# Cached pages loaded with two neighbouring tokens on each partition, the two pages of a block on alternate partitions

## The chip, the cores and the metric

The kernel runs on one core of a Trainium2 chip. The metric is the device time of one execution in microseconds (us). The two timed executions of the kernel before gave 888.59 and 891.32 us, a median of 889.96 us.

## What is computed

One inference step of a one-layer decoder with eight attention heads of 64 and four pooling groups. A prompt of 512 tokens and eight sample sequences of four new tokens each go through the same layer. What bears on this change is the attention of the samples: each sequence has 4096 past tokens in a paged cache, 32 pages of 128 tokens, found through a page table. Two pages form a block of 256 tokens. For each head and query the mean of the keys of a block gates it, the best three of the 16 past blocks are attended, and a relative-position bias is added, which depends on the distance of query and key.

```
past = cache_k[layer, page_table[:, :own * ppb]]            # 8 sequences x 32 pages x 128 tokens x 8 heads x 64
kmean = jnp.mean(past.reshape(DB, own, MOBA_BLOCK, N_HEADS, HEAD_DIM), axis=2)
gate = jnp.einsum('bhtd,bhnd->bhtn', qh, kmean)
_, sel = lax.top_k(gate, n_sel)                              # 3 of 16 blocks
s_sel = einsum('bhcd,bhcnkd->bhcnk', qc, k_sel) * SCALE + bias_tab[h_ix, t5_bucket(rel_s)]
p = softmax(concat([s_sel, s_own]))
out = einsum(p_sel, v_sel) + einsum(p_own, v_own)
```

The bias is bucketed. A key more than 127 or so tokens away falls in the last bucket (31), so of the 32 past pages only the last one has biases that differ from token to token. The sum over keys doesn't depend on the order in which the keys of a page stand, as long as keys, values and biases stand in the same one.

## The kernel before

All arrays are float32. The program has a start (modulation, projections, lines 1060 to 1320 on the engines), the attention of the prompt, the output projection of the prompt, and then the MLP of the prompt in eight chunks of 512 hidden columns, beside which the eight sample sequences' attention runs: while the MLP's chunk `i` is worked on, TensorE scores the keys of one sequence, weighs the values of another, and the loads of a third are under way. Five rounds of this are a hardware loop (`Fori(0, LAST - 2)`); the round before it and those after it are written out. At the end the samples' own MLP runs with weights loaded a second time, 2 MB at a time ("tail" pieces).

The cached pages come through SyncE's queue. `load_block` reads two page numbers from the table, waits until a slot of a ring is free, and issues one DMA for each of the two pages, [128 partitions x 512] each: a partition holds one token, 8 heads x 64, 2048 bytes. There are four slots (`SLOTS`) of two pages (`PPB`) for keys (`k_ring`, in `rw`) and four for values (`v_ring`, in `W`). All 512 such DMAs share one queue with the weights: quarters of `w_up` ([128 x 8 x 128]) and `w_down` ([128 x 4 x 256]), and the tail pieces. A slot of keys is free when VectorE has turned it (`kt_ev`), a slot of values when TensorE has weighed it (`v_used`).

VectorE turns each page of keys in 32x32 squares (`turn_keys`, one STREAM_TRANSPOSE [128 x 512] for each page), TensorE multiplies four pages at a time with the queries (`score_keys`), so that in `sc` a row of 128 lanes (head or query group) holds 1024 columns of scores, 32 for each page and quarter. `scores_out` takes them out of PSUM in two halves, adds the far bias `farr` (one number for each lane) to all columns but the last page's, and `lastr` to those of the last page, columns 480 to 511 of the second half. ScalarE takes the exponential, TensorE turns the probabilities and weighs the values page by page (`weigh_values`).

`lastr` is made once, near the start: TensorE multiplies one-hot bucket rows (the table `last` in the constants `c32`) with the relative-bias table into PSUM bank 4, VectorE masks by quarter and reduces over the four quarters (`bias_out_of_banks`). The constants come to `const32`, 32 partitions of 1536 columns, in one DMA issued from line 455.

The order of the queue is written out by hand: `section(i, u)` issues for each eighth of a round two blocks of keys, two of values and one quarter of weights, each behind its wait.

Of the kernel before, what the change touches and what calls it, by code (L numbers as in the profile page):

```python
# [17 lines left out]
ALU = mybir.AluOpType  # L18
# [3 lines left out]
P = 128  # L22
# [4 lines left out]
DB, DT = 8, 4  # L27
NS = DB * DT
# [11 lines left out]
PPB = 2  # L40
# [10 lines left out]
REV = 2 * P + P - 1  # L51
C32 = {}
_at = 0
for _name, _n in (("ownmask", DB * NS), ("rev", REV + 1), ("far", P), ("last", DT * P), ("own", DT * NS), ("spread", P)):
    C32[_name] = (_at, _at + _n)
    _at += _n
C32_W = _at
# [13 lines left out]
def bucket(n):  # L71
    n = max(n, 0)
    if n < 16:
        return n
    return min(16 + int(math.log(n / 16) / math.log(8) * 16), 31)


def shape_constants():

    c128 = np.zeros((P, C128_W), np.float32)  # L80
    part = {name: c128[:, lo:hi] for name, (lo, hi) in C128.items()}
    part["ident"][:] = np.eye(P)
    part["flip"][:] = np.eye(P)[::-1]
    for g, w in enumerate(WINDOWS):
        part["inv_count"][:, 16 * g:16 * g + 16] = 1.0 / np.minimum(np.arange(16) + 1, w)
    for p in range(P):
        h, g, t = p // 16, p // DT % QUADS, p % DT
        part["fold"][p, p % HT] = 1.0
        part["head"][p, p % HT // DT] = 1.0
        part["token"][p, p % DT] = 1.0  # L90
        part["quad"][p, g] = 1.0
        part["others"][p, 0] = NEG if g else 0.0
        for x in range(QUADS):
            part["same"][p, h * 16 + x * DT + t] = 1.0
            part["cross"][p, x * HT + h * DT + t] = 1.0
        for c in range(CUTS):
            part["qmask"][p, c * 2 * QUADS + c // 2 % 2 * QUADS + p // 32] = 1.0
    for n in range(BLOCKS):
        part["lower"][:, n * BLOCKS:n * BLOCKS + n] = 1.0
    c32 = np.zeros((32, C32_W), np.float32)  # L100
    cmask = np.zeros((NH, REV), np.float32)
    o = C32["rev"][0]
    for i in range(REV):
        rel = 2 * P - 1 - i
        if rel >= 0:
            c32[bucket(rel), o + i] = 1.0
        else:
            cmask[:, i] = NEG
    c32[31, C32["far"][0]:C32["far"][1]] = 1.0
    o = C32["last"][0]  # L110
    for t in range(DT):
        for key in range(P):
            c32[bucket(P + t - key), o + t * P + key] = 1.0
    o = C32["own"][0]
    for t in range(DT):
        for r in range(NS):
            c32[bucket(t - r % DT), o + t * NS + r] = 1.0
    o = C32["spread"][0]
    for r in range(HT):
        c32[r, o + r // DT * 16 + r % DT] = 1.0  # L120
    o = C32["ownmask"][0]
    for row in range(HT):
        for b in range(DB):
            for key in range(NS):
                if key // DT != b or key % DT > row % DT:
                    c32[row, o + b * NS + key] = NEG
    return c128, c32, cmask


def decoder_step(nc, x_prompt, x_sample, cache_k, cache_v, state_pool, page_table, c_prompt, c_sample, w_ada, b_ada,  # L130
# [4 lines left out]
    with ctx:  # L135
        def sb(name, shape, dt=F32):
            return ctx.enter_context(nc.sbuf_tensor(name, shape, dt))
# [69 lines left out]
        rstds = sb("rstds", [P, NS])  # L207
        farb = sb("farb", [P, NH])
        farr = sb("farr", [P, 1])
        lastr = sb("lastr", [P, 32])  # L210
        own = sb("own", [P, DB, NS])
        owncur = sb("owncur", [P, NS])
        ownb = sb("ownb", [HT, NS])
# [31 lines left out]
        c_tok = rw[0:1 + DB, 0:D]  # L245
        vec_rows = rw[0:VECS, 2 * D:2 * D + P]
        st_rows = rw[0:DB * STATE, 2304:2304 + AW]
        const32 = rw[0:32, 3072:3072 + C32_W]
        bias_rows = rw[0:NH, 4864:4864 + REV]
        mask_rows = rw[0:NH, 5376:5376 + REV]  # L250
        relb = rw[0:32, 5888:5888 + NH]
# [2 lines left out]
        relx = rw[0:32, 6144:6144 + 5 * P].rearrange("p (s h g t) -> p s h g t", s=5, h=NH, g=QUADS)  # L254
        relrows = rw[0:32, 6144:6144 + 5 * P].rearrange("p (s r) -> p s r", s=5)
        relown = rw[0:32, 6912:6912 + DT * HT].rearrange("p (s h t) -> p s h t", s=DT, h=NH)
        near_last = cmps[:, 0:P].rearrange("p (g n) -> p g n", g=QUADS)
        ada_sums = [rw[:, 7168:7168 + PIECE], rstd[:, :]]
        qT = gT
        v_tok = rw[:, 0:2048].rearrange("p (t n) -> p t n", t=TT)  # L260
# [16 lines left out]
        def bank(i, parts=P, n=512, off=0):  # L277
            return PS[0:parts, i, off:off + n]
# [165 lines left out]
        def _(sp):  # L444
# [47 lines left out]
            def load_block(cache, ring, landed, b, j, freed=None):  # L492

                slot = j % SLOTS
                _, phys = nc.values_load_multi_w_load_instructions(pages[0:1, bass.ds(b * PAGES + PPB * j, PPB)],
                                                                   engines=[mybir.EngineType.SP])
                if freed:
                    sp.wait_ge(*freed)
                for pg in range(PPB):
                    sp.dma_start(ring[:, slot, pg, :], cache[bass.ds(phys[pg], 1), :, :].rearrange("a p n -> (a p) n"))\  # L500
                      .then_inc(landed[slot], 16)

            def load_keys(b, j, first=False):
# [559 lines left out]
        def _(dve):  # L1063
# [112 lines left out]
            def bias_out_of_banks():  # L1176

                dve.wait_ge(bias_ps, 2)
                dve.tensor_copy(farb[:, :], bank(4, P, NH)).then_inc(bias_ev, 1)
                dve.tensor_copy(farr[:, :], bank(4, P, 1, 16)).then_inc(bias_ev, 1)  # L1180
                dve.tensor_tensor(near_last, bank(4, P, P, P).rearrange("p (g n) -> p g n", g=QUADS),
                                  own_quad[:, :, None].to_broadcast([P, QUADS, 32]), ALU.mult).then_inc(last_raw, 1)
                dve.tensor_copy(ownb[:, :], bank(4, HT, NS, 64)).then_inc(bias_ev, 1)
                dve.wait_ge(last_raw, 1)
                dve.tensor_reduce(lastr[:, :], near_last.rearrange("p g n -> p n g"), AX.X, ALU.add).then_inc(bias_ev, 1)
# [153 lines left out]
            def scores_out(b, half):  # L1339

                dve.wait_ge(qk, UNITS * b + 4 * (half + 1))
                src = bank(2 + half)
                lo, mid, hi = 512 * half, 512 * half + (480 if half else 512), 512 * half + 512
                dve.tensor_reduce(gsum[:, 8 * half:8 * half + 8], src.rearrange("p (u n) -> p u n", u=8), AX.X, ALU.add)
                ins = dve.tensor_scalar(sc[:, lo:mid], src[:, 0:mid - lo], farr[:, 0:1], None, ALU.add)
                if half:
                    ins = dve.tensor_tensor(sc[:, mid:hi], src[:, mid - lo:512], lastr[:, :], ALU.add)
                ins.then_inc(sc_in, 1)
                dve.wait_ge(sc_in, 2 * b + half + 1)
                dve.tensor_reduce(tops[:, 8 * half:8 * half + 8], sc[:, lo:hi].rearrange("p (u n) -> p u n", u=8),  # L1350
                                  AX.X, ALU.max).then_inc(sc_ev, 1)
# [206 lines left out]
        def _(pe):  # L1558
            def mm(out, lhsT, rhs, start=True, stop=True, **kw):
                return pe.matmul(out, lhsT, rhs, start=start, stop=stop, **kw)  # L1560
# [86 lines left out]
                lo = C32["own"][0] + t * NS  # L1647
                mm(bank(4, HT, NS, 64), relown[:, t, :, :].rearrange("p h t -> p (h t)"), const32[:, lo:lo + NS], t == 0, t == DT - 1)
            for t in range(DT):
                lo = C32["last"][0] + t * P  # L1650
                last = mm(bank(4, P, P, P), relrows[:, t, :], const32[:, lo:lo + P], t == 0, t == DT - 1)
            last.then_inc(bias_ps, 1)


# [545 lines left out]
```

## Time and profile of the kernel before

| | |
|---|---|
| timed executions, median (lowest to highest) | 889.96 us (888.59 to 891.32) |
| profiled execution, its time | 896.14 us |
| its span, first to last instruction | 894.3 us |
| mean granted TensorE clock | 0.98 |
| TensorE busy | 838.0 us (94%) |
| VectorE, ScalarE, GpSimd busy | 448.7, 338.0, 292.6 us |
| moved by DMA | 254.02 MB, 284 GB/s on the mean |
| the hardware loop, one round | 66.77 us |

The profiled execution's span is 4 us above the median of the timed ones, so differences are what is carried from one to the other. TensorE's busy time is modelled at the ends of its matmuls; what shows its pace is how long a round of the loop takes. "DMA share" is the mean share of time in which the 16 DMA engines had a packet under way; packets overlap a little, so that it can pass 1.

### The profile page before, as it was taken

What the parts mean: (1) busy time and instruction counts of PE and PEld (TensorE: products, weight loads), DVE (VectorE), ACT (ScalarE), POOL (GpSimd) and SP (SyncE); (2) the same over time, 40 slices, a digit from 0 to 9 for tenths busy, and PEclk for the clock granted to TensorE, in tenths of its full rate; (3) what the DMA queues carried; (4) which work ended last, traced back from release to release, by engine and by line L of the source; (5) the groups of instructions that cost most, each with busy time, mean ns of one, the idle gap of its engine ahead of it and who ended that gap; (6) DMA issues with size and microseconds to landing.
All of it is one profiled execution on the core that took longest, in us unless ns stands there. A gap on an engine that the chain in (4) does not pass through costs nothing.

```text
span 894.3 us, 20195 instructions
## 1 busy us (share of the span) xinstructions
PE 838.0 (94%) x7634; PEld 589.7 (66%) x7634; DVE 448.7 (50%) x845; ACT 338.0 (38%) x701; POOL 292.6 (33%) x191
## 2 busy tenths in 40 slices
PE   5799999898999699999999999999999999997984
PEld 4577786666776176666666676676676675576873
DVE  2743223664777884674674674674674441221222
ACT  4233223787114646136136136036036145133011
POOL 0330003956132444334334334334333353225000
PEclk9899999999999899999999999999999999999998
DMA  9842236595998889999999999999999999899896
GB/s 302 324 154 95 95 115 253 166 337 177 297 312 262 298 279 309 316 315 321 311 316 329 299 321 323 302 310 326 298 325 364 288 309 333 279 326 329 304 397 248
DMA packets 167825, 254.02 MB, mean 284 GB/s; under 512 B 10454, under 2 KB 69419, under 8 KB 167755
## 3 DMA queue, kind: packets, MB, share of 16 engines
q1 hardware_dynamic: 166995, 250.66, 82.9%
q0 software_dynamic: 768, 2.51, 0.8%
q8 instruction: 43, 0.70, 0.3%
q14 instruction: 19, 0.16, 0.0%
HBM read 248.56 MB, written 4.75 MB: 283 GB/s over the span
## 4 chain that ended last, share of the span: by engine, by line
PE 80%; DMA 7%; DVE 6%; issue 2%; ACT 2%; SPq 2%; POOL 0%; DVEq 0%; ACTq 0%
PE PS L1560 77%; DMA W<-in_w_down_dram 3%; DMA W<-in_cache_v_dram 2%; DMA mixT<-in_x_prompt_dram 1%; SPq L500 1%; DMA out_dram<-hT 1%; DVE W L1337 1%; PE PS L1909 1%; PE PS L1783 1%; DMA W<-in_w_up_dram 1%; DVE hT L1116 1%; DVE xT L1405 1%; DVE mixT L1277 0%; DVE stat L1279 0%; POOL hT_split L644 0%
## 5 line engine op out<-in xcount | busy, mean ns | idle before, releaser
L706 POOL TENSOR_TENSOR W_split<-W,W_split 128x1024 fp32r<-128x1024 f32 x72 | 172.3, 2393 | 298.6 <-ACT W_split L866 143.2
L1560 PE MATMUL PS<-gT_split,W_split 128*128 128x512 f32 x576 | 200.9, 408 | 1.0 <-DVE xT L1405 0.2
L1337 DVE STREAM_TRANSPOSE W<-rwT 128x512 f32<-128x512 f32 x256 | 162.6, 681 | 36.5 <-PE PS L1560 22.6
L1560 PE MATMUL PS<-rwT_split,W_split 128*128 128x512 f32 x512 | 175.0, 404 | 0.0
L1560 PE MATMUL PS<-hT_split,W_split 128*128 128x512 f32 x416 | 162.3, 399 | 0.5 <-ACT mixT L939 0.5
L1560 PEld LDWEIGHTS PS<-gT_split,W_split 128*128 128x128 f32 x576 | 109.1, 189 | 53.9 <-DVE xT L1405 17.2
L1560 PEld LDWEIGHTS PS<-rwT_split,W_split 128*128 128x128 f32 x512 | 96.7, 189 | 31.9 <-issue 12.6
L1405 DVE SCALAR_TENSOR_TENSOR xT<-PS,mods,xT 128x512 f32<-128x512 f32 x64 | 47.5, 742 | 110.5 <-PE PS L1560 110.2
L866 ACT ACTIVATE W_split<-W 128x1024 fp32r<-128x1024 f32 x32 | 33.9, 1059 | 179.7 <-DMA W<-in_w_up_dram 179.6
L1560 PE MATMUL PS<-kT_split,W_split 128*128 128x512 f32 x256 | 100.3, 392 | 0.0
L1560 PEld LDWEIGHTS PS<-hT_split,W_split 128*128 128x128 f32 x416 | 79.1, 190 | 16.5 <-issue 1.6
L1560 PE MATMUL PS<-W,smp 128*32 128x512 f32 x512 | 75.6, 614 | 7.8 <-DMA W<-in_cache_v_dram 6.7
L1560 PE MATMUL PS<-mixT_split,W_split 128*128 128x512 f32 x224 | 80.8, 403 | 2.2 <-POOL hT_split L644 2.2
L883 ACT ACTIVATE smp<-PS 32x128 f32<-32x128 f32 x256 | 68.5, 267 | 7.1 <-PE PS L1909 4.3
L1560 PE MATMUL PS<-W,qcur 128*32 128x128 f32 x2048 | 69.0, 275 | 0.0
L1560 PEld LDWEIGHTS PS<-W,qcur 128*32 128x32 f32 x2048 | 52.6, 109 | 24.8 <-issue 20.5
L721 POOL TENSOR_TENSOR kT_split<-kT,gT_split 128x512 fp32r<-128x512 f32 x32 | 42.5, 1328 | 71.1 <-ACT gT_split L967 71.1
L1560 PEld LDWEIGHTS PS<-kT_split,W_split 128*128 128x128 f32 x256 | 48.5, 189 | 7.7
L1560 PEld LDWEIGHTS PS<-mixT_split,W_split 128*128 128x128 f32 x224 | 42.9, 191 | 14.7 <-issue 6.2
L972 ACT ACTIVATE W_split<-W 128x1024 fp32r<-128x1024 f32 x32 | 33.8, 1056 | 42.5 <-DMA W<-in_w_down_dram 42.3
L963 ACT ACTIVATE kT<-PS 128x512 f32<-128x512 f32 x32 | 19.1, 597 | 77.5 <-PE PS L1560 77.5
L1560 PEld LDWEIGHTS PS<-W,smp 128*32 128x32 f32 x512 | 11.3, 108 | 38.3 <-issue 22.5
(273 smaller groups left out, 958.3 us busy)
## 6 DMA issues: line engine op xcount, KB each, us to landing
rwT<-in_cache_k_dram SPq DMA_DIRECT2D x256, 256.0 KB, 4.2
W<-in_cache_v_dram SPq DMA_DIRECT2D x256, 256.0 KB, 4.0
W<-in_w_ada_dram SPq DMA_DIRECT2D x12, 2048.0 KB, 10.3
W<-in_w_up_dram SPq DMA_DIRECT2D x32, 512.0 KB, 5.7
W<-in_w_down_dram SPq DMA_DIRECT2D x32, 512.0 KB, 5.8
W<-in_w_down_dram SPq DMA_DIRECT2D x8, 2048.0 KB, 10.3
rwT<-in_w_up_dram SPq DMA_DIRECT2D x4, 2048.0 KB, 10.0
mixT<-in_w_up_dram SPq DMA_DIRECT2D x4, 2048.0 KB, 11.8
```

Of the source, the lines that this page charges most:

```text
L500: sp.dma_start(ring[:, slot, pg, :], cache[bass.ds(phys[pg], 1), :, :].rearrange("a p n -> (a p) n"))\
L706: pool.tensor_tensor(rows_part(RAW, q, W_split), rows_part(RAW, q), rows_part(HIGH, q, W_split), ALU.subtract).then_inc(w_low, 1)
L721: pool.tensor_tensor(g_lo[:, m, :], kT[:, m, :], g_hi[:, m, :], ALU.subtract).then_inc(g_low, 1)
L866: act.activation(rows_part(HIGH, q, W_split), rows_part(RAW, q), ACT.Copy).then_inc(w_high, 1)
L883: last = act.activation(dst, src, ACT.Copy)
L963: act.activation(kT[:, m, :], bank(5 + m % 2), ACT.Relu).then_inc(relu_ev, 1)
L972: act.activation(rows_part(HIGH, q, W_split), rows_part(RAW, q), ACT.Copy).then_inc(w_high, 1)
L1116: dve.tensor_tensor(hT[:, f, :], xT[:, f, :], bank(7), ALU.mult).then_inc(h_norm, 1)
L1337: dve.transpose(ktb[u % 2][:, :, g, :], k_ring[:, j % SLOTS, pg, :]).then_inc(kt_ev, 1)
L1405: dve.scalar_tensor_tensor(xT[:, m, :], bank(5 + m % 2), mods[:, G2 + m, 0:1], xT[:, m, :], ALU.mult, ALU.add).then_inc(dn_ev, 1)
L1560: return pe.matmul(out, lhsT, rhs, start=start, stop=stop, **kw)
L1783: last = pe.transpose(bank(a % 2, P, P, kt * P), logits[a % LB][:, kt * P:(kt + 1) * P], ident)
```

## The change

A page is now loaded as [64 partitions x 1024]: each partition gets two neighbouring tokens, 4096 bytes that lie together in HBM and in SBUF. Page 0 of a block goes to the even partitions of the slot, page 1 to the odd ones. What the rest of the kernel calls "page" (128 partitions x 512) now holds the first token of each pair from both pages, and the next one the second tokens. Every instruction that reads the ring stays as it is, and the two DMAs of a block still count on one semaphore.

Since the two pages of a block are now mixed over two columns groups, the biases of the last page stand on the odd partitions of both halves of the last block: `last` has 256 columns for each of the four queries instead of 128 (bucket 31 for the even partitions), `lastr` 64 columns instead of 32, and `scores_out` splits at 448 instead of 480. `const32` grows from 1536 to 2048 columns; it now begins at column 2816 of `rw`.

```diff
-for _name, _n in (("ownmask", DB * NS), ("rev", REV + 1), ("far", P), ("last", DT * P), ("own", DT * NS), ("spread", P)):
+for _name, _n in (("last", DT * 2 * P), ("ownmask", DB * NS), ("spread", P), ("rev", REV + 1), ("far", P),
+                  ("own", DT * NS)):
...
-        for key in range(P):
-            c32[bucket(P + t - key), o + t * P + key] = 1.0
+        for p in range(P):
+            for side in range(PPB):
+                at = p // 32 * 64 + side * 32 + p % 32
+                key = p // PPB * PPB + side
+                c32[bucket(P + t - key) if p % PPB else 31, o + t * 2 * P + at] = 1.0
...
-        lastr = sb("lastr", [P, 32])
+        lastr = sb("lastr", [P, 64])
...
-        const32 = rw[0:32, 3072:3072 + C32_W]
+        const32 = rw[0:32, 2816:2816 + C32_W]
...
                 for pg in range(PPB):
-                    sp.dma_start(ring[:, slot, pg, :], cache[bass.ds(phys[pg], 1), :, :].rearrange("a p n -> (a p) n"))\
+                    sp.dma_start(ring[pg:P:PPB, slot, :, :],
+                                 cache[bass.ds(phys[pg], 1), :, :].rearrange("a (p s) n -> (a p) s n", s=PPB))\
                       .then_inc(landed[slot], 16)
...
-                dve.tensor_tensor(near_last, bank(4, P, P, P).rearrange("p (g n) -> p g n", g=QUADS),
-                                  own_quad[:, :, None].to_broadcast([P, QUADS, 32]), ALU.mult).then_inc(last_raw, 1)
+                dve.tensor_tensor(near_last, bank(4, P, 2 * P, 2 * P).rearrange("p (g n) -> p g n", g=QUADS),
+                                  own_quad[:, :, None].to_broadcast([P, QUADS, 64]), ALU.mult).then_inc(last_raw, 1)
...
-                lo, mid, hi = 512 * half, 512 * half + (480 if half else 512), 512 * half + 512
+                lo, mid, hi = 512 * half, 512 * half + (448 if half else 512), 512 * half + 512
...
-                last = mm(bank(4, P, P, P), relrows[:, t, :], const32[:, lo:lo + P], t == 0, t == DT - 1)
+                last = mm(bank(4, P, 2 * P, 2 * P), relrows[:, t, :], const32[:, lo:lo + 2 * P], t == 0, t == DT - 1)
```

No instruction is added, taken away or moved on any engine; shapes change. On SyncE's queue, where the first blocks of keys are issued, the kernel before has these rows (ISA rows set a register for the page's address, TENSOR_LOAD reads the page table):

```order
L495 TENSOR_LOAD pages
L500 ISA
L500 DMA rwT<-in_cache_k_dram 128x512
L500 ISA
L500 DMA rwT<-in_cache_k_dram 128x512
```

and the changed kernel these:

```order
L499 TENSOR_LOAD pages
L504 ISA
L504 DMA rwT<-in_cache_k_dram 64x1024
L504 ISA
L504 DMA rwT<-in_cache_k_dram 64x1024
```

Each DMA has half as many rows of twice the length: both sides merge the two tokens to one row of 1024 numbers.

## Rows read from the trace of the kernel before

**Rows 1.** Busy us (count) by stretch: two of the five rounds of the loop.
```profile
core 0: us, PE busy (x) PEld busy (x) DVE busy (x) ACT busy (x) POOL busy (x), PEclk, DMA share, GB/s
339.64:406.40 66.76, 66.61 (x538) 45.24 (x538) 39.41 (x70) 25.45 (x54) 25.31 (x14) 1.00 0.94 310
...
606.70:673.47 66.77, 66.62 (x539) 45.26 (x538) 39.16 (x70) 25.46 (x54) 25.43 (x14) 1.00 0.94 316
```

**Rows 2.** Stretches from the output projection to the loop, columns as in rows 1.
```profile
260.00:300.00 40.00, 35.67 (x363) 24.00 (x361) 30.95 (x54) 13.15 (x28) 7.15 (x3) 0.96 0.88 283
300.00:340.00 40.00, 34.34 (x234) 19.86 (x235) 33.77 (x55) 25.40 (x49) 22.88 (x15) 0.91 0.87 287
```

**Rows 3.** Who TensorE waited for, 219 to 345 us: us, times, longest.
```profile
PE PS L1560 <- DMA W<-in_cache_v_dram: 6.7, 3, 3.5
```

**Rows 4.** The chain that ended last: start us, us, what.
```profile
275.88 5.38 DMA W<-in_w_up_dram
...
296.95 5.29 DMA W<-in_cache_v_dram
...
307.59 3.89 DMA W<-in_cache_v_dram
...
733.09 10.22 DMA W<-in_cache_v_dram
```

**Rows 5.** DMA issues: count, KB each, median us from issue to landing.
```profile
W<-in_w_down_dram SPq DMA_DIRECT2D x8, 2048.0 KB, 10.3
rwT<-in_w_up_dram SPq DMA_DIRECT2D x4, 2048.0 KB, 10.0
mixT<-in_w_up_dram SPq DMA_DIRECT2D x4, 2048.0 KB, 11.8
```

**Rows 6.** Stretches of the tail, columns as in rows 1.
```profile
860.00:865.00 5.00, 4.58 (x113) 4.15 (x106) 0.66 (x3) 1.79 (x5) 0.00 (x0) 1.00 1.05 392
865.00:870.00 5.00, 3.42 (x108) 2.62 (x100) 2.73 (x4) 1.19 (x3) 0.00 (x0) 1.00 1.02 403
870.00:875.00 5.00, 3.08 (x73) 2.65 (x73) 2.03 (x4) 1.69 (x4) 0.00 (x0) 1.00 1.05 390
```

**Rows 7.** SyncE's issues in the tail: start us, us, what.
```profile
852.41 0.37 SPq L578 DMA_DIRECT2D rwT<-in_w_up_dram  x1
860.12 0.37 SPq L578 DMA_DIRECT2D W<-in_w_down_dram  x1
861.86 0.37 SPq L578 DMA_DIRECT2D mixT<-in_w_up_dram  x1
```

**Rows 8.** Stretches near the start, columns as in rows 1.
```profile
10.00:11.20 1.20, 1.09 (x4) 0.72 (x4) 0.00 (x0) 1.11 (x2) 0.00 (x0) 1.00 1.02 402
11.80:13.00 1.20, 0.79 (x4) 0.39 (x2) 0.00 (x0) 0.81 (x2) 0.00 (x0) 1.00 1.04 171
13.00:14.00 1.00, 0.00 (x0) 0.00 (x0) 0.00 (x0) 0.00 (x0) 0.00 (x0) 1.00 0.99 195
18.00:20.00 2.00, 2.00 (x12) 1.95 (x10) 0.56 (x4) 0.25 (x1) 0.00 (x0) 1.00 1.05 387
```

**Rows 9.** SyncE's issue of the constants: start us, us, what.
```profile
7.50 0.40 SPq L455 DMA_DIRECT2D rwT<-in_shape_c_dram  x1
```

**Rows 10.** Timeline around the bias matmuls: start us, us, what [idle before, releaser].
```profile
33.10 3.07 PE L1560 MATMUL PS<-rwT 32*8 32x383 f32 x22
37.37 0.77 PE L1560 MATMUL PS<-mixT_split,W_split 128*128 128x512 f32 x1 [1.19 <-POOL hT_split L644]
...
34.47 0.63 ACT L800 ACTIVATE mixT_split<-hT 128x512 fp32r<-128x512 f32 x1 [3.04 <-DVE hT L1160]
...
44.59 0.29 DVE L1125 COPY rwT<-PS 128x128 f32<-128x128 f32 x1 [3.25 <-PE PS L1560]
```

**Rows 11.** Groups on VectorE in one round: count, busy us, mean ns.
```profile
L1345 DVE TENSOR_SCALAR scn<-PS,farr 128x480 f32<-128x480 f32 x1 | 0.7, 707 | 0.0
...
L1347 DVE TENSOR_TENSOR scn<-PS,lastr 128x32 f32<-128x32 f32 x1 | 0.2, 178 | 0.0
```

More of the change, by code:

```diff
@@ L256, in decoder_step @@
         relown = rw[0:32, 6912:6912 + DT * HT].rearrange("p (s h t) -> p s h t", s=DT, h=NH)
-        near_last = cmps[:, 0:P].rearrange("p (g n) -> p g n", g=QUADS)
+        near_last = cmps[:, 0:2 * P].rearrange("p (g n) -> p g n", g=QUADS)
         ada_sums = [rw[:, 7168:7168 + PIECE], rstd[:, :]]
@@ L1649, in _ @@
             for t in range(DT):
-                lo = C32["last"][0] + t * P
-                last = mm(bank(4, P, P, P), relrows[:, t, :], const32[:, lo:lo + P], t == 0, t == DT - 1)
+                lo = C32["last"][0] + t * 2 * P
+                last = mm(bank(4, P, 2 * P, 2 * P), relrows[:, t, :], const32[:, lo:lo + 2 * P], t == 0, t == DT - 1)
             last.then_inc(bias_ps, 1)
```

## The prediction

> **What bounds the kernel now.** I read the page's busy times and slices first, then the busy time by stretch, then TensorE's waits, the chain that ended last and the DMA issues.
>
> TensorE is the bound almost everywhere. A round of the hardware loop takes 66.77 us, TensorE is busy 66.6 of them, and rounds that lie 267 us apart agree to 0.01 us [rows 1]. A pace set by transfers would not repeat so closely, since their rate differs from round to round (310 and 316 GB/s). The reader should see two more things there. VectorE is busy 39 us of a round, so it is far from the bound. And the DMA engines are busy 0.94 of the round: the loads are hidden, but without much room. In a round a sequence's keys and values move, 64 pages of 262,144 bytes, 16.78 MB, and 4.19 MB of weights; 20.97 MB in 66.77 us is 314 GB/s, as the rows say.
>
> The cached pages show on TensorE in one place only, between the output projection and the loop. From 260 to 340 us TensorE is idle 4.33 + 5.66 = 10.0 us [rows 2], and 6.7 us of its waits from 219 to 345 us are for values [rows 3]. The chain has three transfers there, of 5.38, 5.29 and 3.89 us; the first is a quarter of weights queued behind pages [rows 4]. A fourth, of 10.22 us at 733 us, ends in TensorE work that had no gap ahead of it, so it is worth nothing. The start and the tail load no pages.
>
> **The change part by part.**
>
> *Rows of 4096 bytes instead of 2048.* 512 DMAs keep their bytes and have half the rows. The nearest rows are in the tail, where `w_down` (4096-byte rows) and `w_up` (2048-byte rows) take turns, both with a full queue. A `w_up` piece is issued at 852.41 us, a `w_down` piece at 860.12, a `w_up` piece at 861.86 [rows 7]. By the bytes ahead of each, they move about from 860 to 865, 865 to 870 and 870 to 875 us. The rates are 392, 403 and 390 GB/s [rows 6]: 403 / 391 = 1.031. From issue to landing the pieces take 10.3 us for `w_down` and 10.0 or 11.8 us for `w_up` [rows 5], which bounds the gain between -3% and +13%. I take 3.1%, since those stretches compare full queues directly.
>
> On the path this counts only in the three transfers of the opening: 5.38 + 5.29 + 3.89 = 14.56 us, and 3.1% of it is 0.5 us. The bounds are 14.56 x -0.03 = 0.4 us lost and 14.56 x 0.13 = 1.9 us gained. In the loop the DMA share falls from 0.94 to about 0.92 and TensorE's matmuls cover it: 0 us. If that cover were gone, if a round were bound by DMA, a round would gain 3% of 16.78 MB / 391 GB/s = 42.9 us, 1.4 us.
>
> *Half the partitions for each DMA.* This is the part no row of before shows, since every large load there fills 128 partitions. The nearest rows speak of a cost. The constants are a load on 32 partitions only, issued at 7.50 us [rows 9], behind 2 MB of the prompt and so due at about 12 us. Just there, with the DMA share at 1.04 and 0.99, only 171 and 195 GB/s move, against 387 at the same share a little later [rows 8]. The engines had work and were held up at the other end: rows that crowd into part of the partitions move at half rate. Which partitions the sixteen DMA engines write at one moment decides. Every second partition from 0 to 127 reaches the same parts of SBUF as all 128, so on the mean nothing crowds; whether two engines meet at one moment can't be read. The bounds are 387 GB/s (no loss) and 195 (all meet). I take no loss as the likelier: just ahead of the constants the queue carries `state_pool`, a load of 120 rows of 2048 bytes, which isn't dealt as 128 rows are either, and the stretch before 11.2 us still moves at full rate [rows 8]. It is the main rival below.
>
> The Trainium skill (SBUF — State Buffer, Door 1: The DMA port swizzle) says that bandwidth goes by how many of 16 ports the partitions reach, and that partitions 0 to 63 reach only eight. The slow stretch at the constants agrees with it (171 to 195 against 387 GB/s). By that rule alternate partitions reach all sixteen ports and the loss is 0; the page doesn't say how rows two partitions apart are dealt to the engines, and had the two pages stood on partitions 0 to 63 and 64 to 127, it would speak for half rate.
>
> *Larger constants.* 32 x 512 x 4 = 65,536 bytes more at 171 to 195 GB/s delay what is queued behind, the first weights, by 0.34 to 0.38 us. ScalarE, which splits these weights, is idle 3.04 us before its next operation, and that waits for VectorE [rows 10]. So 0; 0.4 us if the cover were gone.
>
> *Bias matmuls.* Four matmuls of 128 columns become four of 256. The 22 matmuls around them take 3.07 us, 0.14 us each, most of them narrower; doubling four costs between 0.14 x 4 = 0.6 and, at the 0.77 us that a 128 x 512 one takes, half of it, 0.39 x 4 = 1.5 us. TensorE then waits 1.19 us for GpSimd [rows 10]. I take 0.6 and so 0 on the path; the worst is 0.3 us. VectorE masks and reduces twice as many columns once; it is idle 3.25 us soon after [rows 10]: 0.
>
> *The scores.* For each sequence one instruction loses 32 columns of 480 (707 ns, at most 47 ns less) and one gains 32 (178 ns for 32, so at most 178 more) [rows 11]. Behind them in VectorE's queue stand the turning of keys and the ranking, and VectorE has 27 us of a round to spare: 0.
>
> **Sum.** 894.3 - 0.5 = 893.8 us for the span of the profiled execution. That span is 4.3 us above the median of the timed ones, 889.96; carried over, **889.5 us**. By the bounds this case runs from 889.96 - 1.9 = 888.1 to 889.96 + 0.4 + 0.4 + 0.3 = 891.1; with the scatter of the two timed executions, 1.4 us each way, 886.7 to 892.5.
>
> **The rivals.**
>
> *Engines meet (slower).* If a DMA of 64 rows two partitions apart is dealt so that two engines write the same part of SBUF at the same time, pages move slower. A round has 66.77 us and its weights need 4.19 MB / 390 GB/s = 10.7 us, so pages must keep 16.78 MB / 56.0 us = 300 GB/s; below that DMA becomes the bound of every round. At half rate (195) a round takes 86.1 + 10.7 = 96.8 us, 30 more; over the eight sequences 240 us, about 1130 us. If they meet half of the time, the rate is about 258 GB/s, a round takes 65.0 + 10.7 = 75.7 us, 9 more, and with seven such rounds about 63 us, 953 us. For it: the half rate at the constants. Against it: all sixteen parts are reached, and engines that start apart stay apart. I give it 0.21.
>
> *The rows are cut to 2048 bytes again (no effect).* Then nothing moves faster: 890.0 us. For it: no row of before has such a DMA of pages. Against it: the queue's rows say 64 x 1024, and `w_down` has rows of that length with a visible rate of its own. 0.20.
>
> *Much faster pages.* If the longer rows brought all pages of the opening ahead of TensorE, its 10.0 us of idle time there [rows 2] would go: 880 us. Against it: half of that time is other waits, and the rows give 3%. 0.03. The Trainium skill (Perfetto Trace Analysis, DMA Optimizations) says that going from 2 KB to 4 KB can "dramatically improve throughput"; the tail's rows, 391 against 403 GB/s, don't agree. Even that rule would meet a loop bound by TensorE, hence 880 us.
>
> *The forecast* itself has 0.56.
>
> **How the numbers follow.** The predicted time is that of the likeliest case, 889.5 us. The first case, the second rival and the third all lie between 880 and 893; the slow rival holds 0.21, and its mildest part, a rate just below 300 GB/s, begins there too: I put the upper end at 910 us, which leaves out 0.19. What 2% means, 17.8 us, is about what a measurement of this kernel can tell from no change. Faster by more is ruled out but for 0.02, since the idle time that pages could give back is 10 us; slower by over 2% is the slow rival, 0.20; within it 0.78. The likeliest case's own range is 886.7 to 892.5.
>
> **What would show it.** Right: half as many packets for the pages, rounds of 66.8 us, a DMA share a little lower, waits for values of 6 to 6.7 us in the opening, rates of 310 to 317 GB/s in the loop. Wrong: rounds over 67 us with TensorE waiting for pages, a DMA share at 1 with under 300 GB/s (engines meet); as many packets as before (cut rows); TensorE idle after the bias matmuls for GpSimd by nothing and the next projection later (uncovered start).

## The result and the profile after

The changed kernel takes **912.44 us**, the median of two executions (911.17 to 913.72), against 889.96 before: 22.5 us more, a ratio of 1.021 with a 95% interval of 1.016 to 1.026. Run again on another chip, four executions against 13 of the kernel before, it was 1.023 (1.0185 to 1.0275; `after_again` below). So it is slower, by about 2%, where 889.5 us was forecast, and the time lies 2.4 us above the upper end of the range. Times and ratios leave out executions more than 1.5% above the fastest of the same kernel, of which only `halves` had any.

The profiled execution has a span of 911.9 us against 894.3. That is 17.6 us, less than the 22.5 between the medians, since the profiled execution of the kernel before took 896.14 us, 6 more than its median. The stretches below run from one start of `rstd<-PS,rden,cst` on VectorE to the next: it stands once in a round, so these are the rounds, first of the kernel before (columns as in rows 1):

```profile
414.18:480.94 66.76, 66.61 (x549) 45.26 (x541) 39.43 (x68) 25.45 (x55) 25.32 (x14) 1.00 0.94 317
681.24:744.46 63.22, 62.74 (x410) 42.20 (x399) 27.59 (x49) 23.40 (x52) 23.27 (x12) 1.00 0.95 322
```

and of the changed kernel:

```profile
349.75:416.52 66.77, 66.62 (x549) 45.25 (x541) 41.06 (x69) 24.98 (x54) 23.63 (x14) 1.00 0.92 303
416.52:484.65 68.13, 66.98 (x549) 45.38 (x541) 39.69 (x68) 24.27 (x54) 24.87 (x13) 1.00 0.92 303
484.65:553.13 68.48, 66.69 (x549) 45.25 (x541) 39.66 (x68) 24.96 (x55) 25.36 (x13) 1.00 0.92 305
553.13:624.95 71.82, 69.46 (x549) 46.62 (x541) 37.77 (x68) 27.40 (x57) 28.18 (x14) 0.98 0.91 305
624.95:691.72 66.77, 66.62 (x549) 45.25 (x541) 39.24 (x69) 23.95 (x53) 23.29 (x13) 1.00 0.92 304
691.72:764.21 72.49, 65.23 (x410) 43.81 (x399) 27.62 (x49) 24.86 (x54) 25.30 (x12) 0.95 0.90 312
```

The opening up to 349.75 is 2.3 us longer (347.41 before), the five rounds take 341.97 us instead of 333.83, 8.1 more, the stretch after them 72.49 instead of 63.22, 9.3 more, and the rest 2.1 less: 17.6 in all. In the stretch of 72.49 us TensorE is idle 7.3 us, where it was idle 0.5, and busy 2.5 us longer, at a granted clock of 0.95 instead of 1.00. Where [rows 1] had rounds equal to 0.01 us, three of the five differ now. TensorE isn't the bound there: in the third round it is busy 66.7 of 68.5 us. The DMA engines aren't either: their share fell to 0.92 and they move 303 to 305 GB/s where they moved 317. Nothing that the prediction held for a possible bound is one.

The one that is busy all the time is SyncE, which issues the pages. First who SyncE waited for from 339.64 to 673.47 us, five rounds of the kernel before (us in total, times, longest), then the row of its page issues before (one of its two buffers: duration ns min/median/max, first and last start us):

```profile
SPq L500 <- PE PS L1560: 24.9, 24, 2.9
SPq L500 <- DVE W L1337: 8.4, 5, 1.9
...
L500 SPq DMA_DIRECT2D rwT<-in_cache_k_dram x256: 328/333/1661, 215.5 to 692.6; - x128
```

The same row of the changed kernel, and how long its page loads took from issue to landing, min/median/max:

```profile
L504 SPq DMA_DIRECT2D rwT<-in_cache_k_dram x256: 474/475/1047, 216.2 to 709.5; - x128
...
DMA to landing us min/median/max: 2.8/4.0/12.6
```

Issuing one page costs SyncE **475 ns instead of 333**. A round has 64 of them: 64 x 0.142 = 9.1 us. In the five rounds before SyncE waited 24.9 + 8.4 = 33.3 us, 6.7 in each; its work was 60.1 us of 66.8. It becomes 69.2, more than TensorE's 66.6. The profile after has no wait of SyncE at all from 340 to 600 us. The transfers themselves didn't slow down: from issue to landing the median is 4.0 us, against 4.1 before.

SyncE's own round can be read without any sum. It issues the first quarter of `w_up` once in each round of the loop, in the changed kernel at these times (start us, us, what):

```profile
435.25 0.38 SPq L518 DMA_DIRECT2D W<-in_w_up_dram  x1
504.20 0.38 SPq L518 DMA_DIRECT2D W<-in_w_up_dram  x1
573.17 0.38 SPq L518 DMA_DIRECT2D W<-in_w_up_dram  x1
642.15 0.38 SPq L518 DMA_DIRECT2D W<-in_w_up_dram  x1
```

That is 68.95, 68.97 and 68.98 us, while TensorE's rounds took between 66.77 and 71.82. SyncE goes at one pace and TensorE, with the slots of the rings between the two, follows unevenly. A round of 66.77 us on TensorE doesn't mean that SyncE kept up in it.

Downstream it shows as later landings of all that SyncE issues. VectorE's waits for keys from 340 to 600 us, before:

```profile
DVE W L1337 <- DMA rwT<-in_cache_k_dram: 5.4, 2, 2.7
```

and after:

```profile
DVE W L1342 <- DMA rwT<-in_cache_k_dram: 70.4, 35, 4.7
```

VectorE, which turns the keys, waits for them 35 times instead of 2. It has 27 us of a round to spare and hides much of that. What reaches TensorE from 340 to 765 us, where the kernel before has one wait of 0.2 us, comes by two roads in the main:

```profile
PE PS L1565 <- DVE xT L1410: 5.5, 2, 5.3
PE PS L1565 <- POOL qcur L703: 4.8, 3, 2.2
```

The first is about keys. The chain that ended last runs from 632 to 696 us along SyncE's own instructions, one behind the other, then over a transfer of keys to VectorE, where an operation of the MLP (`xT`, for which TensorE waits) stands behind the turning of these keys:

```profile
696.37 12.45 DMA rwT<-in_cache_k_dram
708.85 1.30 DVE W L1342 x2
710.15 0.64 DVE xT L1410
```

The second is about weights, which come through the same queue. ScalarE waits for a quarter of `w_up`, GpSimd for ScalarE, and the queries (`qcur`) of the next sequence stand behind that on GpSimd:

```profile
588.41 1.06 ACT L871 ACTIVATE W_split<-W 128x1024 fp32r<-128x1024 f32 x1 [8.69 <-DMA W<-in_w_up_dram]
589.55 2.39 POOL L711 TENSOR_TENSOR W_split<-W,W_split 128x1024 fp32r<-128x1024 f32 x1 [7.35 <-ACT W_split L871]
591.88 1.04 POOL L703 TENSOR_TENSOR qcur<-qrep,cst 128x512 f32<-128x512 f32 x1
593.06 1.94 PE L1565 MATMUL PS<-W,qcur 128*32 128x128 f32 x32 [2.19 <-POOL qcur L703]
```

A wait can cost more than its length. In the round from 553 to 625 us TensorE waits only 2.2 us, yet it is busy 2.8 us longer. The granted clock had been 1.00 (2.4 GHz) and fell to a mean of 0.87 and then 0.71, between that level and 1.2 GHz, in the stretches that hold the gap and follow it:

```profile
590.00:594.00 4.00, 1.81 (x24) 1.28 (x26) 2.92 (x5) 0.00 (x0) 2.93 (x2) 0.87 0.90 283
594.00:598.00 4.00, 4.00 (x31) 3.00 (x24) 0.55 (x1) 1.06 (x1) 0.76 (x1) 0.71 0.97 341
```

In the two rounds before, with 1.2 and 1.8 us of idle time, the clock stayed at 1.00.

### The profile page after: what moved, and what is told of

It reads as the page before. It is cut to its first block, busy times and chain, and to the rows that moved or that the text cites. A ratio compares the mean times of both kernels' runs of the same rounds, so it can differ in the third digit from the quotient of the medians.

```text
span 911.9 us, 20195 instructions
## 1 busy us (share of the span) xinstructions
PE 845.2 (93%) x7634; PEld 593.0 (65%) x7634; DVE 449.8 (49%) x845; ACT 337.7 (37%) x701; POOL 293.3 (32%) x191
## 2 busy tenths in 40 slices
DMA packets 135057, 254.09 MB, mean 279 GB/s; under 512 B 10454, under 2 KB 69419, under 8 KB 134955
## 4 chain that ended last, share of the span: by engine, by line
PE 41%; issue 24%; DMA 9%; SPq 9%; POOL 8%; DVE 6%; ACT 3%; POOLq 0%; DVEq 0%; ACTq 0%
PE PS L1565 39%; SPq L504 6%; POOL W_split L711 5%; DMA rwT<-in_cache_k_dram 3%; DMA W<-in_w_down_dram 3%; SPq L499 2%; POOL kT_split L726 2%; DMA W<-in_cache_v_dram 2%; DVE W L1342 1%; DMA mixT<-in_x_prompt_dram 1%; DMA W<-in_w_up_dram 1%; PE PS L1788 1%; ACT mixT L898 1%; DVE hT L1121 1%; DVE mixT L1282 1%
## 5 line engine op out<-in xcount | busy, mean ns | idle before, releaser
L1342 DVE STREAM_TRANSPOSE W<-rwT 128x512 f32<-128x512 f32 x256 | 164.5, 686 | 120.3 <-DMA rwT<-in_cache_k_dram 107.1
L1565 PE MATMUL PS<-W,smp 128*32 128x512 f32 x512 | 77.7, 612 | 8.3 <-DMA W<-in_cache_v_dram 7.4
L1565 PE MATMUL PS<-W,qcur 128*32 128x128 f32 x2048 | 69.9, 278 | 5.2 <-POOL qcur L703 4.8
```

Of the source, the lines that this page charges most:

```text
L1342: dve.transpose(ktb[u % 2][:, :, g, :], k_ring[:, j % SLOTS, pg, :]).then_inc(kt_ev, 1)
```

## The experiments

The theory is that the changed rows cost SyncE 0.142 us more for each page, and that this alone, against 6.7 us to spare, makes the loss. The rivals are that the layout in SBUF slows the transfers (the prediction's slow rival), and that something else of the change (the bias, the scores) does it.

**The issue by itself.** `probe_issue` is the kernel before with bursts of eight loads behind the last output, one shape to a burst.

> The kernel before, with bursts of eight loads of cache pages added at the very end of SyncE's queue, each burst behind a wait for the one before: [128 x 512] as before, [64 x 1024] on every second partition as in the changed kernel, [64 x 1024] on one half of the partitions, [64 x 512] on every second partition, [64 x 512] on one half, [128 x 256], and [128 x 1024]. Theory S (SyncE pays for the issue): the issue of the [64 x 1024] load on every second partition takes 475 ns as in the trace of the changed kernel, that of [128 x 512] 333 ns; whichever of the others also takes 475 tells whether it is the step of two partitions, the number of rows or their length. Theory C (DMA engines meet in the same part of SBUF): the burst on every second partition lands clearly later than that of [128 x 512], by up to twice for 2 MB (about 5.4 us at 387 GB/s against 10.8 at half rate), and that on one half of the partitions is at half rate for sure. If both are small the issue alone is left.

```profile
L647 SPq DMA_DIRECT2D rwT<-in_cache_k_dram x8: 333/360/381, 889.8 to 893.5; - x8
...
L650 SPq DMA_DIRECT2D rwT<-in_cache_k_dram x8: 538/546/603, 898.4 to 902.9; - x8
...
L659 SPq DMA_DIRECT2D rwT<-in_cache_k_dram x8: 485/546/547, 925.7 to 930.1; - x8
```

L647 is a load of 128 rows of 512 numbers, L650 of 64 rows of 1024 on every second partition, L659 of 64 rows of 512 on 64 neighbouring partitions. The other two bursts of 64 rows (1024 numbers on neighbouring partitions, 512 on every second) have a median of 546 ns too, and 128 rows of 256 and of 1024 numbers 381 and 432. So 64 rows cost 546 ns whatever their length and wherever they go, and 128 rows 360 to 432: the price hangs neither on the step of two partitions nor on the bytes, and it is the smaller load that costs more. (Behind the kernel an issue is dearer than inside the loop, by 27 to 116 ns over this run and the next.)

**How many rows.** `probe_rows`, made the same way, has bursts of four loads with rows of 512 numbers, 128, 112, 96, 64, 32 and 16 of them, and then bursts of 1 MB loads.

> The kernel before with bursts of four loads at the very end of SyncE's queue, each behind a wait for the burst before: 128, 112, 96, 64, 32 and 16 rows of [512] from the cache, then loads of 1 MB: [128 x 4 x 512], [128 x 2 x 1024], [64 x 4 x 1024] on every second partition, the same on one half of the partitions. Issue: 128 rows at about 0.36 us, 64 rows at about 0.54; if the cost goes with the number of rows in a plain way it changes step by step, if 128 is a case of its own all others cost about 0.5. Transfer: with the issue out of the way, theory C has every second partition at half rate (10 us and more for 4 MB beyond the full-rate 10.8 us), its rival at the full rate; one half of the partitions alternating should be slower than the full rate.

```profile
L639 SPq DMA_DIRECT2D rwT<-in_cache_k_dram x4: 356/432/435, 893.2 to 894.5; - x4
...
L645 SPq DMA_DIRECT2D rwT<-in_cache_k_dram x4: 313/426/427, 904.1 to 905.4; - x4
...
L648 SPq DMA_DIRECT2D rwT<-in_cache_k_dram x4: 567/591/598, 908.8 to 910.7; - x4
```

That is 128, 96 and 64 rows; 112 rows cost 427 ns, 32 rows 366, 16 rows 420. Only 64 stands out, by 160 to 225 ns. Nothing grows or shrinks with the count. In all these loads the number of rows is also the number of partitions. The 1 MB loads that follow part the two: one of 256 rows costs 368 to 712 ns on 128 partitions and 611 to 974 on 64. With four issues each, scattered as they are, that points to the partitions and doesn't prove it. Why 64 is a case of its own was not found.

The bursts of 1 MB loads show the transfer without the issue as a limit. Busy time by stretch, columns as in rows 1, in this order: 128 partitions with rows of 2048 bytes, 128 partitions with rows of 4096, every second partition, and the two halves in turn:

```profile
920.03:933.40 13.37, 0.00 (x0) 0.00 (x0) 0.00 (x0) 0.00 (x0) 0.00 (x0) 0.50 0.84 314
933.67:946.00 12.33, 0.00 (x0) 0.00 (x0) 0.00 (x0) 0.00 (x0) 0.00 (x0) 0.50 0.88 340
946.19:959.40 13.21, 0.00 (x0) 0.00 (x0) 0.00 (x0) 0.00 (x0) 0.00 (x0) 0.50 0.86 318
959.63:981.00 21.37, 0.00 (x0) 0.00 (x0) 0.00 (x0) 0.00 (x0) 0.00 (x0) 0.50 0.95 196
```

Each stretch holds the latency of one burst, so only their ratios count. Every second partition moves at 318 GB/s, against 340 for rows of the same length on 128 partitions and 314 for the old rows; that is nowhere near half, and so the engines don't meet. The 6% to 340 are 0.9 us, and SyncE also spends 0.9 us more on issuing that burst. The halves in turn move at 196.

**Only the values.** In `values_only` the keys keep the old load, and the rest of the change is undone with them; the values are loaded as the change loads them.

```diff
+                    if cache is cv:
+                        sp.dma_start(ring[pg:P:PPB, slot, :, :],
+                                     cache[bass.ds(phys[pg], 1), :, :].rearrange("a (p s) n -> (a p) s n", s=PPB))\
...
+                    else:
+                        sp.dma_start(ring[:, slot, pg, :], cache[bass.ds(phys[pg], 1), :, :].rearrange("a p n -> (a p) n"))\
...
```

> The kernel before with only the values' pages loaded as [64 x 1024] on every second partition; keys, scores and biases as before (the values are then weighed by the probabilities of other tokens, the amount of work is the same). Theory S: SyncE has 33.3 us of waits in five rounds of the loop, 6.7 a round; 32 value DMAs a round cost 32 x 0.142 = 4.5 us more, which fits, so the rounds stay at 66.77 us and the whole within 0.5% of the kernel before (889 to 894 us). Theory C: half of the pages collide, so half of the loss stays: about 900 us.

It takes 896.84 us (891.02 to 899.74) against 891.92 on the same chip, a ratio of 1.005 (1.003 to 1.008). Its rounds are 66.80 us long, and this is all that SyncE waited from 345 to 600 us:

```profile
SPq L501 <- PE PS L1565: 6.8, 6, 1.7
```

That is 1.8 us for each round. From 6.7 less 32 x 0.142 = 4.5 one would have 2.2. Half of the dearer issues fit under TensorE in the loop, as the budget says. The whole is 4.9 us slower than the kernel before all the same, 2.8 above the upper end that was expected; where these lie was not traced.

**Giving SyncE the time back.** `after_wide` is the changed kernel, but in the loop it reads the page numbers of two blocks at a time, so 16 of the 32 reads of a round fall away. The loads stay as they are.

```diff
+                k_pages = read_pages(kb, PPB * ku, 2) if keys else None
+                v_pages = read_pages(vb, PPB * vu, 2) if values else None
...
-                        load_keys(kb, PPB * ku + half)
+                        load_keys(kb, PPB * ku + half, phys=k_pages[2 * half:2 * half + 2])
```

> The changed kernel, but in the eight sections of a round SyncE reads four page numbers at once instead of two twice, 16 reads of the page table a round fewer (0.47 us each, 7.6 us a round). Theory S: SyncE's excess of 9.1 - 6.7 = 2.4 us a round is gone, rounds are 66.8 us again, the whole is back at 889 to 892 us. Theory C: reading page numbers faster changes nothing in how the loads move, about 912 us.

It takes 899.81 us (895.15 to 901.70), ratio 1.008 (1.005 to 1.011): most of the loss is gone, but not all, and it is above the 889 to 892 us that were expected. The round is whole again, and SyncE waits (340 to 600 us):

```profile
484.43:551.23 66.80, 66.65 (x549) 45.25 (x541) 39.60 (x68) 25.38 (x55) 25.45 (x14) 1.00 0.92 311
```

```profile
SPq L510 <- PE PS L1574: 30.9, 21, 3.7
SPq L510 <- DVE W L1351: 5.0, 3, 1.9
```

The issue still costs 474 to 475 ns, DMA moves at a share of 0.92, and the bias and the scores are the changed ones: of all that the change did, only SyncE's budget was touched, and the loop's loss is gone. The stretch after the five rounds is back at 63.7 us, from 72.49. The medians are still 8 us apart, the profiled executions 899.8 - 894.3 = 5.5. Of these 3.4 lie in the opening (up to 350.83 against 347.41) and 2.0 in the stretch from the seventh start of that operation on VectorE to the eighth (748.51 to 786.16, before 744.46 to 780.11), where numbers were still read one block at a time.

**The same everywhere, in both kernels.** `after_wide_all` and `before_wide_all` read the numbers of two blocks at a time in the opening and for the last sequence as well. They differ from each other by the change under study alone.

```diff
+            def values_at(b, j, blocks, first=False):
+                two = None
+                for n in range(blocks):
+                    if n % 2 == 0:
+                        two = read_pages(b, j + n, min(2, blocks - n))
+                    load_values(b, j + n, first, two[PPB * (n % 2):PPB * (n % 2) + PPB])
```

> The changed kernel with page numbers read for two blocks at once everywhere: also in the opening and for the last sequence, where the run after_wide still read two at a time. Theory S: what was left there (3.4 us up to the first round's mark and 2.5 us among the last values) goes, 890 to 894 us. Rival: the loads themselves land later, 897 us and more.

> The kernel before with page numbers read for two blocks at once everywhere. Theory S: SyncE had waits to spare in the loop, so the rounds stay at 66.77 us; in the opening its queue is part of the chain (about 5% of 121 us), so 0 to 4 us are gained: 886 to 892 us.

896.45 us (894.56 to 902.06) and 896.44 (891.45 to 898.58), beside 894.63 for the kernel before: ratios of 1.003 (1.000 to 1.005) and 1.002 (1.000 to 1.005). The first lies between what the theory (890 to 894) and its rival (897 and more) expected, the second above its 886 to 892. What decides is the pair: on the same chip their medians differ by 0.01 us, ten executions each. With room on SyncE the change is worth nothing, neither way. SyncE's waits from 340 to 600 us, `after_wide_all` first:

```profile
SPq L510 <- PE PS L1580: 29.7, 21, 3.7
SPq L510 <- DVE W L1357: 7.2, 4, 2.1
```

```profile
SPq L506 <- PE PS L1575: 62.3, 27, 4.8
SPq L506 <- DVE W L1352: 11.0, 4, 2.9
```

36.9 us in 260 are 9.5 in a round of 66.8, 73.3 are 18.8. The difference, 9.3 us a round, is the 64 x 0.142 = 9.1 us once more, now between two kernels that both have time for it. Neither version beats the kernel before: what `before_wide_all` saves on SyncE isn't on the path there.

These waits are longer than 16 reads of 474 ns can explain, and the row of the read says why. Reading two page numbers takes 474 ns, reading four (`before_wide_all`) takes less:

```profile
L494 SPq TENSOR_LOAD <-pages x128: 293/299/701, 213.8 to 767.0; - x128
```

So `after_wide`, with 9.2 us of waits a round and 57.6 us of work instead of 69.2, gains 16 x 0.474 = 7.6 us by the reads that fall away and 16 x 0.175 = 2.8 by those that stay, 10.4 of 11.6.

**The same load on SyncE without the change.** If SyncE's time is the cause, the kernel before must slow down when SyncE alone gets more to do. The three `delay` kernels are the kernel before with page numbers read a second time for some of the 8 residues of the block's number; `delay_quarter`, whose edit is shown, adds 8 reads of about 470 ns to a round, `delay_half` 16 and `delay_only` 20.

```diff
+                if j % 8 in (0, 5):
+                    _, again = nc.values_load_multi_w_load_instructions(pages[0:1, bass.ds(b * PAGES + PPB * j, PPB)],
+                                                                        engines=[mybir.EngineType.SP])
+                    phys = (phys[0], again[1])
```

> The kernel before with its loads of pages unchanged ([128 x 512], rows of 2048 bytes) but with a second read of the page table for five blocks in eight, which lets SyncE's queue spend 0.474 x 5/8 = 0.30 us more on a block, against 2 x 0.142 = 0.28 us in the changed kernel. Theory S (SyncE's time for the issue is the whole cause): the loss of the changed kernel is there without any change in a load: 909 to 914 us, rounds of the loop of 66.8 to 69.5 us, no waits of SyncE in the loop. Rival (the shape of the load costs something in the transfer too): it stays clearly below 908 us.

> As delay_only, with the second read for four blocks in eight. In delay_only a second read cost SyncE more than its own 0.47 us: rounds were 74.9 us with SyncE never waiting, 14.8 us above its 60.1 us of work a round in the kernel before, 0.74 us for each of 20 reads. Theory S: 16 reads cost 8 to 11.8 us a round, against 6.7 us to spare, so rounds of 68 to 72 us and 905 to 925 us in all, about the loss of the changed kernel, with every load as in the kernel before. Rival (the changed kernel's loss comes from its loads' way through the DMA engines): nothing of it is here, about 895 us.

> As delay_only, with the second read for two blocks in eight: 8 reads cost 4 to 5.9 us a round, less than the 6.7 us that SyncE has to spare. Theory S: rounds stay at 66.8 us and the whole within 0.7% of the kernel before; a loss in proportion to the reads (8/20 of 44 us, 17 us) would speak against the picture of a spare time that has to be used up first.

`delay_only`: 938.31 us (937.93 to 939.87), ratio 1.049 (1.045 to 1.053), rounds of 74.9 us. `delay_half`: 927.36 us (922.16 to 931.01), ratio 1.041 (1.038 to 1.044), rounds of 73.7. `delay_quarter`: 894.02 us (891.24 to 899.64), ratio 1.001 (0.998 to 1.003), rounds of 66.8 with SyncE waiting a little:

```profile
SPq L504 <- PE PS L1564: 8.5, 11, 1.4
SPq L504 <- DVE W L1341: 2.5, 3, 1.0
```

Every load is as in the kernel before. SyncE has no wait from 340 to 600 us in `delay_half` and `delay_only`, and the loop slows down to SyncE's pace. In `delay_quarter` 2.8 us of waits a round are left, so a read took (6.7 - 2.8) / 8 = 0.49 us, its row and little more, and the loop is whole.

The two slow ones came out slower than expected (`delay_half` 905 to 925, `delay_only` 909 to 914 us). The row of an added read is no longer there than in `delay_quarter` (medians of 468 to 470 ns), and reads of 0.49 us would give less: 60.1 + 16 x 0.49 = 67.9 us and 60.1 + 20 x 0.49 = 69.9. Most of the rest is one pause in each round, where SyncE's loop turns. The last issue of a round and the first of the next, in `delay_half` and then in `delay_quarter`:

```profile
558.40 0.39 SPq L521 DMA_DIRECT2D W<-in_w_down_dram  x1
565.52 0.85 SPq L504 DMA_DIRECT2D rwT<-in_cache_k_dram  x2
...
539.02 0.38 SPq L521 DMA_DIRECT2D W<-in_w_down_dram  x1
540.63 0.85 SPq L504 DMA_DIRECT2D rwT<-in_cache_k_dram  x2
```

7.1 us against 1.6. From the loop's branch to the next instruction pass 4.2 to 5.3 us in `delay_half`, 3.1 to 4.6 in `delay_only`, and 0.20 to 0.25 in `delay_quarter`, the kernel before and the changed one. A turn of the loop has 327 and 331 instructions on SyncE in the first two, 319 in `delay_quarter` and 311 in the kernels before and after. What it does in the pause isn't shown; the 0.74 us a read that was expected for `delay_half` was this pause shared out over the reads. So these kernels show the mechanism: 8 reads cost nothing while there is time to spare, and time taken from SyncE alone slows the loop. They show neither the size of the loss nor where exactly the spare time ends, since at 16 reads only about 1 us of the 7 that a round lost is the reads'. The size is shown by the issue rows, SyncE's rounds of 69.0 us and the wide kernels.

**The pages on halves of the partitions.** In `halves` a block's pages stand on partitions 0 to 63 and 64 to 127, with the bias in that order. The rows and their number are those of the change.

```diff
-                    sp.dma_start(ring[pg:P:PPB, slot, :, :],
+                    sp.dma_start(ring[P // PPB * pg:P // PPB * (pg + 1), slot, :, :],
```

> The changed kernel with page 0 of a block on partitions 0 to 63 and page 1 on 64 to 127 (biases placed to suit), rows of 4096 bytes as in the changed kernel. Theory S: if the step of two partitions makes the issue dear, it is back at 333 ns and the loop at 66.8 us unless transfers bind; if the rows do, it stays 475 ns and about 912 us. Theory C in its strong form: each load now crowds into half of SBUF's parts, the rate falls towards 195 GB/s when loads do not overlap, rounds of 75 us and more, over 950 us in all.

It takes 1028.74 and 1031.07 us in the two executions that count, a ratio of 1.155 (1.153 to 1.158). The profiled one took 1056.45 us; one of its rounds:

```profile
464.22:551.98 87.76, 76.54 (x546) 50.01 (x538) 38.32 (x68) 25.26 (x54) 25.24 (x13) 0.92 1.06 239
```

Here DMA is the bound: a share of 1.06 at 239 GB/s, where the change has 0.92 at 303. This is what transfers that crowd look like, and the changed kernel looks otherwise. The Trainium skill (SBUF — State Buffer, Door 1: The DMA port swizzle) says that partitions 0 to 63 reach eight of sixteen ports. This trace and the burst of halves (196 against 318 GB/s) agree.

**The change once more.** `after_again` is the changed kernel with nothing edited.

> The changed kernel once more beside the two delays, on the same chip. 909 to 916 us; the ratio to the kernel before with a narrower interval, about 1.02.

It takes 914.41 us (909.24 to 917.79) against 893.06, ratio 1.023 (1.0185 to 1.0275). The profiled execution has rounds of 66.8, 70.4, 66.8, 68.8 and 69.5 us: a loss like the first one, in other rounds. SyncE's own rounds, read at the same issue as above, are 68.96, 68.98 and 68.96 us again.

## Why the prediction was wrong

*What bounds the kernel now.* Right as far as it went: TensorE was the bound, and DMA was hidden. But the list of what stands close behind was short by one. I read TensorE, VectorE and the DMA share [rows 1], and never SyncE, which isn't in the busy columns. Its waits said that only 6.7 us of a round were free, a tenth.

*"512 DMAs keep their bytes and have half the rows."* This is **the step that failed**. It priced a DMA by its transfer alone and took the issue as unchanged. That the change moves no instruction was taken as if each would cost what it had. The missing term is 64 x 0.142 = 9.1 us a round on an engine with 6.7 to spare. With it the sum is 69.2 - 66.8 = 2.4 us for each full round; measured, SyncE's round is 69.0, 2.2 more than TensorE's. The five rounds on TensorE lost 1.6 each on the mean (8.1 / 5), part of SyncE's lag being carried on into the stretch after them. That stretch lost 9.3 us, which the sum doesn't give: 6.8 of idle time, the wait behind the late keys above all, and 2.5 at a lower clock. With SyncE's time given back it is 63.7 us in `after_wide`. That the range ended only 2.4 us short of the result is luck: its upper end of 910 was set by the rival of engines that meet, which didn't happen.

I could not have read 475 ns from the trace, but could have bounded it: the issues of 2 MB weight loads take 0.37 us [rows 7] and the one on 32 partitions 0.40 [rows 9], against 0.333 for a page. At 0.40 the term is 4.3 us, within the spare time, and at twice the price 21 us. The point where it decides, 6.7 / 64 = 0.105 us more for each issue, would have been a rival with a condition and a price, and the range would have reached past 912.

*In the loop 0 us, "TensorE's matmuls cover it".* Right for the transfer, wrong for the round. The DMA share fell from 0.94 to 0.92, as said.

*Half the partitions for each DMA; the rival of engines that meet.* The value taken, no loss, was right: 318 against 314 and 340 GB/s in the bursts, and an unchanged landing time. The rival's price was right in kind: in `halves` DMA is the bound of the rounds. I had given it 0.21, and in fact the slower outcome came by another road, which had no rival.

*Rows cut again; much faster pages.* Neither came: 135,057 packets instead of 167,825, and the opening didn't become shorter.

*The opening.* 0.5 us was forecast to be gained, and the transfers give no sign of it that can be told from scatter: TensorE's waits for values are 6.7 us before [rows 3], 5.8 in the changed kernel and 9.0 in `after_again`, which is the same kernel. The opening as a whole is 2.3 us longer. SyncE's issues are the likely reason, not a shown one. From the first page's issue to the first round's mark pass 131.9 us before, 133.6 and 134.5 in the two profiles of the changed kernel, and 129.1 in `after_wide_all` against 129.9 in `before_wide_all`, where SyncE has room; but in `delay_half` and `delay_only`, where SyncE has more to do than before, it is 128.0 and 132.2.

*The bias matmuls.* The term was 0.6 us with 1.5 as its bound, and the cover 1.19 us [rows 10]. After:

```profile
33.37 3.91 PE L1565 MATMUL PS<-rwT 32*8 32x383 f32 x22
37.64 0.76 PE L1565 MATMUL PS<-mixT_split,W_split 128*128 128x512 f32 x1 [0.36 <-POOL hT_split L649]
```

3.91 - 3.07 = 0.84 us more, and the wait for GpSimd shrank from 1.19 to 0.36, as the step said it would. What follows starts 0.27 us later than before (37.64 against 37.37), and that isn't the matmuls' doing: the group itself already starts 0.27 us later (33.37 against 33.10 [rows 10]). Whether the larger constants did this, priced at 0 with 0.4 us as the bound, isn't shown.

*The scores.* Right: the operation on 448 columns takes 674 ns instead of 707 for 480 [rows 11], the one on 64 columns 216 instead of 180 for 32.

*The Trainium skill* (DMA: Bandwidth & Descriptors, Issuing engines are not separate DMA queues) says that the sequencer's time for initiating a DMA "is usually small relative to the DMA itself". For one load this trace agrees, 0.475 us against 4.0 to landing. For the queue it doesn't help: 64 issues and 32 reads fill the round while the transfers overlap.

## What to carry to other kernels

Whoever changes the shape of a DMA may change what its issue costs: count the issuing engine's work in a round (round less its waits) as one counts TensorE's, and compare the spare time with the number of DMAs times what one may get dearer. Where an issuing engine runs close, a read of a page number or a second small load is what to save first, but only a saving on the path shows. A change that adds and moves no instruction can still move the bound.

## What the runs showed of the hardware

- A load of 64 rows on 64 partitions costs SyncE more to issue than one of 16, 32, 96, 112 or 128 rows: 475 ns against 333 in the loop, 546 to 591 against 360 to 432 behind the kernel. Length and partition step don't matter. The 1 MB loads point to the 64 partitions and not to the 64 rows. The reason wasn't found.
- Loads on every second partition moved at 318 GB/s, loads on all 128 at 314 and 340, and loads on halves in turn at 196.
- Reading four page numbers has a shorter row on SyncE than reading two, 299 ns against 474.
- SyncE's loop pauses for 3.1 to 5.3 us at each turn where it has 327 or 331 instructions, and for 0.20 to 0.25 us where it has 311 or 319. What it does there isn't shown.
